# A decoder trunk on one NeuronCore: the roots of the head norms spread over the partitions by DMA instead of by matmul

## The reference, cut to what matters

```python
def _head_rmsnorm(y, g, n_heads):
    b, l, w = y.shape
    yh = y.reshape(b, l, n_heads, w // n_heads)
    yh = yh * lax.rsqrt(jnp.mean(yh * yh, axis=-1, keepdims=True) + NORM_EPS)
    return yh.reshape(b, l, w) * g.astype(F32)
...
    gates = jax.nn.sigmoid(merge_logits.reshape(b, l, N_BRANCH, D_MODEL) + b_merge.astype(F32))
    branches = (y_sb, y_gla, y_ml, y_ret)
    merged = gates[:, :, 0] * (branches[0] @ w_branch[0].astype(F32))
    for n in range(1, N_BRANCH):
        merged = merged + gates[:, :, n] * (branches[n] @ w_branch[n].astype(F32))
```

## Time and profile before

| | |
|---|---|
| Time, median of 3 runs | 978.7 us (978.58 to 979.68) |
| The profiled execution | 978.57 us |
| Its span in the trace | 976.4 us |
| Mean granted clock of TensorE | 0.998 |
| PE busy | 99% of the span |
| DVE busy | 60% |
| ACT busy | 52% |
| POOL busy | 8% |
| DMA queue of SP (q1) | 51% of 16 engines |

### The profile page before, as it was taken

One profiled execution on the slowest core, in us unless ns is written; L12 is line 12 of the kernel. 1 busy time (PEld: TensorE's weight loads), 2 busy tenths in 40 slices (PEclk: granted clock), 3 DMA queues, 4 the chain that ended last, 5 costly groups with the idle time before them and its releaser, 6 DMA issues.

```text
span 976.4 us, 19018 instructions
## 1 busy us (share of the span) xinstructions
PE 963.8 (99%) x7450; PEld 908.1 (93%) x7450; DVE 590.7 (60%) x894; ACT 512.5 (52%) x822; POOL 79.6 (8%) x72
## 2 busy tenths in 40 slices
PE   8999999999999999999999999999999999999998
PEld 6999888899999999999979999888999899999886
DVE  7566575367857655553456675654679566665543
ACT  6543744475466544444445546544754765544542
POOL 1000000000031222210100000000000312122000
PEclk9999999999999999999999999999999999999999
DMA  6875334346562655555544664433465635656652
GB/s 192 279 231 161 118 115 130 112 125 161 164 208 73 194 172 172 173 182 183 156 129 147 186 184 130 131 113 117 143 180 167 191 122 182 194 191 195 213 174 86
DMA packets 164299, 158.02 MB, mean 162 GB/s; under 512 B 9603, under 2 KB 157294, under 8 KB 163854
## 3 DMA queue, kind: packets, MB, share of 16 engines
q1 hardware_dynamic: 163118, 153.76, 51.0%
q10 hardware_dynamic: 928, 3.33, 1.0%
q0 software_dynamic: 192, 0.07, 0.0%
HBM read 154.98 MB, written 1.05 MB: 160 GB/s over the span
## 4 chain that ended last, share of the span: by engine, by line
PE 92%; DVE 4%; ACT 2%; DMA 1%; issue 1%; ACTq 0%; DVEq 0%; SPq 0%
PE banks L684 24%; PE banks L686 24%; PE banks L685 24%; PE banks L1059 2%; PE banks L1061 2%; PE banks L1060 2%; PE banks L734 2%; PE banks L719 1%; PE banks L715 1%; PE banks L716 1%; DVE lo L1521 1%; PE banks L926 1%; PE banks L924 1%; DVE term L1817 1%; PE banks L664 1%
## 5 line engine op out<-in xcount | busy, mean ns | idle before, releaser
L684 PE MATMUL banks<-xh,hi 128*128 128x272 f32 (+1 forms) x1584 | 457.2, 289 | 0.2
L1521 DVE TENSOR_TENSOR lo<-raw,hi 128x1024 fp32r<-128x1024 f32 (+1 forms) x288 | 349.0, 1215 | 174.1 <-ACT hi L1146 173.6
L686 PE MATMUL banks<-xh,lo 128*128 128x272 f32 (+1 forms) x1584 | 452.9, 286 | 0.0
L685 PE MATMUL banks<-xl,hi 128*128 128x272 f32 (+1 forms) x1584 | 451.9, 285 | 0.0
L1146 ACT ACTIVATE hi<-raw 128x1024 fp32r<-128x1024 f32 (+1 forms) x288 | 301.6, 1048 | 118.5 <-PE banks L686 43.2
L684 PEld LDWEIGHTS banks<-xh,hi 128*128 128x128 f32 x1584 | 298.5, 188 | 6.6 <-issue 4.7
L686 PEld LDWEIGHTS banks<-xh,lo 128*128 128x128 f32 x1584 | 298.6, 189 | 0.0
L685 PEld LDWEIGHTS banks<-xl,hi 128*128 128x128 f32 x1584 | 298.3, 188 | 0.0
L1236 ACT ACTIVATE gates<-banks,par 128x272 f32<-128x272 f32 (+1 forms) x64 | 30.7, 480 | 98.2 <-PE banks L686 91.1
L1967 POOL TENSOR_TENSOR silu_g<-silu_g,rstd 128x272 f32<-128x272 f32 (+1 forms) x44 | 54.6, 1240 | 216.7 <-ACT silu_g L1411 216.7
L1960 POOL TENSOR_TENSOR sq<-sq 128x272 f32<-128x272 f32 (+1 forms) x18 | 21.3, 1185 | 608.6 <-ACT sq L1396 608.0
(11 more groups left out here) (272 smaller groups left out, 1253.3 us busy)
## 6 DMA issues: line engine op xcount, KB each, us to landing
raw<-in_w_in SPq DMA_DIRECT2D x54, 1024.0 KB, 5.2
raw<-in_ffn_w_gate SPq DMA_DIRECT2D x22, 1024.0 KB, 5.3
raw<-in_ffn_w_up SPq DMA_DIRECT2D x22, 1024.0 KB, 5.3
raw<-in_ffn_w_down SPq DMA_DIRECT2D x19, 1024.0 KB, 5.1
raw<-in_w_out SPq DMA_DIRECT2D x8, 1024.0 KB, 5.1
raw<-in_w_in SPq DMA_DIRECT2D x12, 512.0 KB, 4.2
raw<-in_w_branch SPq DMA_DIRECT2D x12, 512.0 KB, 5.4
raw<-in_ffn_w_down SPq DMA_DIRECT2D x4, 768.0 KB, 4.4
```

Of the source, the lines that this page charges most:

```text
L684: mm(dst, wh, mh, start=start, stop=False)
L685: mm(dst, wh, ml, start=False, stop=False)
L686: return mm(dst, wl, mh, start=False, stop=stop)
L1521: tt(half_of(lo, g, c), half_of(raw, g, c), half_of(hi, g, c).bitcast(F32), ALU.subtract).then_inc(lo_ready, 2 if g in G_MIX else 1)
```

## The change

The selector matrix, its 768 columns of constants and the function `headbc` go away. In their place SP gets the function `spread_norms`. It waits for the roots, writes them by four DMAs (three rows of 272 numbers each) into a scratch `norm_rows` in device memory, waits until these have landed, and reads them back by four DMAs, each with a source that is repeated over 64 partitions, into a new SBUF tile `spread` of 128 x 6 x 272. `spread` lies where `pt` was, which is free once the last mixer's values are done (`o_ready`). `y_rest` waits for all four reads and takes `spread` from SBUF instead of a PSUM bank.

```diff
-          ("headsum", 3 * 32), ("headbc", 6 * P), ("denind", 32), ("negind", 4)]
+          ("headsum", 3 * 32), ("denind", 32), ("negind", 4)]
...
-    19: [("headbc",)],
...
+        (spread,), _ = tenants(merged_at, [("spread", [P, 6, T], F32)])
+        norm_rows = nc.dram_tensor("norm_rows", (DEPTH, HEADS, 3, T), F32, kind="Internal").ap()
...
+            def spread_norms(l):
+                sp.wait_ge(hrstd_ready, l + 1)
+                for g in range(HEADS):
+                    sp.dma_start(norm_rows[l, g], M["rows"][32 * g:32 * g + 3, 0, :]).then_inc(norm_moved, 16)
+                sp.wait_ge(norm_moved, 128 * l + 64)
+                sp.wait_ge(o_ready[l], 8)
+                for i in range(2):
+                    rows = slice(HD * i, HD * i + HD)
+                    sp.dma_start(spread[rows, 0:2, :], norm_rows[l:l + 1, i::2, 0, :].broadcast_to((HD, 2, T))).then_inc(norm_moved, 16)
+                    sp.dma_start(spread[rows, 2:6, :], norm_rows[l:l + 1, :, 1 + i, :].broadcast_to((HD, 4, T))).then_inc(norm_moved, 16)
...
                     load(G_LOGIT[l] + j // 2, wm[:, :, C_MERGE + n * D + m * P:C_MERGE + n * D + m * P + 256])
+                spread_norms(l)
                 for k in range(6):
...
-            def headbc(l):
-                pe.wait_ge(hrstd_ready, l + 1)
-                pe.wait_ge(sc_free[l], 4 * HEADS)
-                pe.wait_ge(ex_free[l], 2 * HEADS)
-                pe.wait_ge(k0_free[l], 4)
-                pe.wait_ge(den_abs, l + 1)
-                pe.wait_ge(o_free[l], 8)
-                for p in range(6):
-                    rows = slice(HD * p, HD * p + HD) if p < 2 else quad[p - 2]
-                    mm(spread_banks[p][:, 0:T], c3("headbc", 6)[rows, p, :], M["rows"][rows, 0, :], start=True, stop=True).then_inc(spread_ready[l], 1)
...
-                dve.wait_ge(spread_ready[l], p + 1)
-                stt(osb[:, n, q0:], osb[:, n, q0:], par[:, l, row + n % 2:row + n % 2 + 1], spread_banks[p][:, q0:T],
+                dve.wait_ge(norm_moved, 128 * l + 64 + 64)
+                stt(osb[:, n, q0:], osb[:, n, q0:], par[:, l, row + n % 2:row + n % 2 + 1], spread[:, p, q0:],
```

More of the change, by code:

```diff
@@ L89 @@
           ("decay", 4 * SCW), ("decay0", T), ("cos", T), ("sin", T),
-          ("headsum", 3 * 32), ("headbc", 6 * P), ("denind", 32), ("negind", 4)]
+          ("headsum", 3 * 32), ("denind", 32), ("negind", 4)]
 CONST_FIRST = 257
 CONST_W = sum(w for _, w in CONSTS)
-def head_row(pair, i):
-    return 32 * (2 * pair + i) if pair < 2 else 32 * (pair - 2) + 1 + i
 def constants():
@@ L131, in constants @@
     c["headsum"][:HD, 64 + 1] = c["headsum"][HD:, 64 + 2] = 1.0 / HD
-    for pair in range(6):
-        for i in range(P):
-            c["headbc"][head_row(pair, i // HD), pair * P + i] = 1
     c["denind"][:, 0] = 1
@@ L441, in turn_banks @@
             return (ops, k0) if name == "sbv" else (sc[0], sc[1])
-        spread_banks = [banks[:, 2 + p, :] for p in range(6)]
         branch_banks = [banks[:, 2 + 2 * i:4 + 2 * i, :] for i in range(3)]
@@ L459, in build @@
         row_summed = sq_ready[DEPTH - 1][3]
-        pair_done = sem("pair_done")
+        pair_done, norm_moved = sem("pair_done"), sem("norm_moved")
         ss_ready = sem("ss_ready")
@@ L465, in build @@
         names = """
-            rot_sin spread_ready spread_free sq_summed
+            rot_sin spread_free sq_summed
             silu_ready silu_scaled rstd_ready xn_ready xh_ready xl_ready post_scaled h_ready pad_set
@@ L472, in build @@
             ml_ready ah_ready al_ready turn_ready turn_free""".split()
-        (rot_sin, spread_ready, spread_free,
+        (rot_sin, spread_free,
          sq_summed, silu_ready, silu_scaled, rstd_ready, xn_ready, xh_ready, xl_ready, post_scaled, h_ready,
@@ L989, in _ @@
             parts = {
-                "first": first, "group": group, "turn": turn, "gate": gate, "logit": logit, "headsum": headsum, "headbc": headbc,
+                "first": first, "group": group, "turn": turn, "gate": gate, "logit": logit, "headsum": headsum,
                 "sb_scores0": sb_scores0, "sb_scores": sb_scores,
```

## The result

The changed kernel takes 994.21 us (median of 4 runs, 993.27 to 995.0), the kernel before 979.19 us beside it: a ratio of 1.0148, 95% interval 1.0136 to 1.0161. It is slower, as forecast, but by 15 us in place of 5.4. The profiled execution took 993.27 us; its span is 991.0 us, 14.6 more than before.

What follows compares the result with a forecast made beforehand. PE was taken as the bound, busy for 963.8 of 976.4 us. To 978.57 us the prediction added 1.5 and 2.3 for the longer layers, net of the gain, and 1.6 for the clock: 984.0 us, range 979.5 to 989.5.

Steps and rivals of the forecast that it cites:

- gain on PE: Logits 19 to 20, both layers: without the spread and its break PE gains 2 x 1.53 = 3.06 us.
- load issued to writes landed, layer 0: SP's queue: load issued at 200.96, the small writes behind it landed at 206.6, 0.5 us behind the load.
- reads: Four DMAs of together 836 KB into the spread tile: 4.8 us, bounds 4.2 and 6.5.
- tile to logit 20 taken: Layer 0, DVE and ACT: logit 20 is taken 2.94 us after the spread tile is there.
- standstills of PE: Ahead of logit 22: PE stands still 3.0 us in layer 0 and 3.9 us in layer 1.
- clock: Behind the standstills: one fall to the 1.2 GHz level for both layers, 1.6 us; bounds none and 3.2.
- the longer trip with two falls: Rival: writes at 207.4, reads of 6.5 us, tile at 213.9 and about 702.8, two falls; 990.6 us, chance 0.13.
- The hidden trip: Rival: tile there at 208.4 and 696.4, PE waits for nothing and the gain is whole; 975.5 us, chance 0.09.

Runs made afterwards that it cites:

- the kernel without a trip: Changed kernel without the eight DMAs, y_rest multiplying by a tile of ones once the roots are ready; 977.51 us, 0.9982 of the kernel before.
- the unused trip: Kernel before, selector matmuls kept, with the same eight DMAs added at the same place and only the much later merge waiting for them; 979.7 us, 0.9999.
- all ahead: Changed kernel with all eight DMAs issued ahead of the weight load of logits 24 and 25 in place of behind it; 983.41 us, 1.0045.
- plain source: Changed kernel with reads of the same shapes from 64 different rows of a weight matrix in place of the repeated scratch row; 992.35 us, 1.0125.
- two reads: Changed kernel with two reads in contiguous pieces of 6528 bytes in place of four, and eight small writes in place of four; 993.23 us, 1.0147.
- on POOL's queue: Changed kernel with all eight DMAs of the trip issued by POOL in place of SP, shapes and order unchanged; 990.07 us, 1.0112.
- half of the bytes: Changed kernel with its four reads cut to half their size, pairs of heads sharing rows; 987.9 us, 1.0094.
- first pairs first: Changed kernel with the reads for pairs 0 and 1 issued first, on their own semaphore, for which y_rest 0 and 1 wait; 984.91 us, 1.0053.
- POOL, first pairs first: Changed kernel with the trip on POOL's queue and the first two pairs' reads first, on their own semaphore; 983.6 us, 1.0039.
- all ahead, first pairs first: Changed kernel with all eight DMAs ahead of the load of logits 24 and 25 and the first two pairs read first, with their own wait; 982.8 us, 1.0027.
- writes ahead: Changed kernel with the four writes ahead of the load of logits 24 and 25 and the reads behind it, first pairs first; 979.96 us, 1.0003.
- writes and first pairs ahead: Changed kernel with writes, their wait and reads of pairs 0 and 1 ahead of the load of logits 24 and 25, other reads behind; 979.24 us, 0.9997.
- the run with matmuls of ones: Changed kernel with nine calls of the function that issues matmuls of ones on PE ahead of logit 22; 987.53 us, 1.0078.

## Why the prediction was wrong

The sign and the mechanism were right, a wait of PE at logit 22 in each layer and a slow clock behind it, and the sizes were not: 993.27 us for the profiled execution against 984.0, above the range. By its own terms:

| term | forecast | measured in the profile |
|---|---|---|
| gain on PE | 3.06 | 2.1 (976.4 - 974.3, the kernel without a trip) |
| load issued to writes landed, layer 0 | 5.6 | 5.9 |
| reads | 4.8 | 6.6 and 6.85 |
| tile to logit 20 taken | 2.94 | 2.81 |
| standstills of PE | 3.0 and 3.9 | 5.0 and 5.6 |
| clock | 1.6 | 6.0 |

**What the prediction saw.** PE followed from logit 22 on without standing still again. The loads weren't hurt, which the unused trip shows best. The writes landed 0.7 behind the load (forecast 0.5), and the packets show the reason that the text had, the place behind the load in SP's queue. The chain from the tile to the bank was right to 0.13 us.

**The reads: the first step that failed.** They were sized at 4.8 us, with 6.5 as the upper bound, and took more than that bound. The value was read off between the rows for 512 KB (4.2) and 1024 KB (5.1), which differ by 0.9 us for half a megabyte. The four issues were then counted only in the upper bound. Half the bytes show that these reads have a steeper slope, 1.7 and 1.3 us for 418 KB, and the rate row shows them at 184 to 264 GB/s where the weight load reaches 400, with the DMA engines as busy. The upper bound was itself built on the 512 KB row; the 6.2 us of the gain vector (a row of the view of all DMAs, not of the page) were at hand, for fewer bytes than the tile has, and were read only as the absence of a slow repetition. The runs exclude the repeated source, and larger pieces in fewer reads account for 0.7 to 0.9 us. What else nearly halves the rate stays open. With the writes, 0.3 us later against the load than forecast, the standstills become 3.7 us longer than forecast.

**The clock: the second step, and the larger.** The size of one fall was right: four stretches at the half level cost 6.0 us of busy time, 1.5 each, where 1.6 stood in the forecast. The number of falls was wrong. The text took one for both layers, with two as the upper bound, because the only row at hand showed a single stretch of 3.4 us; behind standstills of 5.0 and 5.6 us there were two stretches each. Either step alone would have stayed inside the range, 984.0 + 3.7 = 987.7 and 984.0 + 4.4 = 988.4; together they leave it. And they hang together: over the runs, the longer waits have the more stretches, though not one by one, for 3.2 us in one layer brought none and 2.2 us in another brought one. (All columns are in us; in the two rows "all ahead" the waits are those of all logit tiles of the layer.)

| kernel | waits at logit 22, layers 0 and 1 | at half clock | PE busy above 961.1 |
|---|---|---|---|
| changed | 5.0, 5.6 | 6.8, 6.8 | 6.0 |
| plain source | 5.3, 5.6 | 6.8, 6.8 | 5.5 |
| two reads | 5.1, 5.6 | 6.8, 6.8 | 5.0 |
| on POOL's queue | 5.1, 5.6 | 3.4, 6.8 | 3.4 |
| half of the bytes | 3.4, 4.4 | 3.4, 3.4 | 3.5 |
| first pairs first | 3.2, 3.2 | 0, 3.4 | 2.4 |
| POOL, first pairs first | 2.6, 3.0 | 0, 3.4 | 1.5 |
| all ahead | 2.5, 2.5 | 3.4, 0 | 2.3 |
| all ahead, first pairs first | 1.3, 2.2 | 0, 3.4 | 3.1 |
| writes ahead | 2.1, 1.1 | 0, 0 | 0.5 |
| writes and first pairs ahead | 0.7, 0.4 | 0, 0 | 1.2 |

The last column holds more than the clock, as the last two rows show (0.5 and 1.2 us without any fall), so the 1.5 per stretch is good to some tenths only; the run with matmuls of ones gives 6.7 / 4 = 1.7 by the medians and 5.4 / 4 = 1.4 by the profiled executions.

The Trainium skill, TensorE: Matmul & The Clock Gate, section "What's actually happening", has the half rate as the default that activity releases. The run with matmuls of ones agrees: the same 10.9 us of delay, no fall, 6.7 us less. The prediction quoted it and priced it at one fall more, so two in all, where four came.

**The gain.** The break between logits 19 and 20 was 1.53 us in each layer, and its removal brought 2.1 us of span and 2.0 of time. The term itself was sized right, since the logit tiles are 1.5 us shorter in each layer. The 1.0 us by which the span falls short lies elsewhere, 0.35 of it ahead of logit 18 of layer 0, 0.2 between the layers and 0.4 behind logit 26 of layer 1. The medians fall short by as much, so it isn't an accident of one profile; no run shows where it comes from.

**The rivals.** The nearest was the longer trip with two falls, 990.6, at a chance of 0.13: its tile at 213.9 for 214.44. Its clock term, too, was half of what came. The hidden trip had the estimate from the Trainium skill, DMA: Bandwidth & Descriptors, section "Anatomy of one DMA", of 5.9 us for writes and reads together. The section fits its 2.0 us and 436 GB/s to DMAs issued by GpSimd, which the prediction didn't say, and the trip here is issued by SP. Measured were 5.9 us from the load's issue to the landing of the writes alone, and 6.6 for the reads. Where nothing else was in flight, the four writes took 2.2 us from the first issue, and the last of them, issued at 202.60, had landed at most 1.2 us later, sooner than the page's 2.0 us; on POOL's queue beside a load they took 3.3 to 4.7 us each, more than it.

With the terms as measured the sum is 978.57 - 2.1 + 10.6 + 6.0 = 993.1 us, against 993.27. That is bookkeeping of the same profiles; what tests it are the run in which nobody waits and the one with matmuls of ones.

## What to carry to other kernels

Before a round trip through device memory takes the place of a broadcast on an engine, write down when its first and its last byte are needed: here the same eight DMAs cost 15 us against the kernel before where one wait was set for all of them behind a 1 MB load, and nothing where the writes and the first consumer's part stood ahead of that load and the rest behind it. Price a wait of PE together with the slow stretch behind it, since 10.6 us of waiting cost 16.6 here. And measure first what there is to gain: the kernel without any trip was only 2.0 us faster, so that even a well placed trip ended level.

## What the runs showed of the hardware

- Four DMAs of 3 KB issued on SP's queue right behind a 1 MB load moved as the load's last packets ran, and had landed 5.9 us after the load's issue; with no load in flight they took 2.2 us from the first issue. From POOL's queue, beside the load, the first landed after 3.3 us, ahead of the load, and the others after 4.4 to 4.7 us each.
- Four reads of together 836 KB, each over 64 partitions in pieces of 1088 bytes, ran at 184 to 264 GB/s where a load of 1 MB over 128 partitions reached 400 GB/s, with the DMA engines as busy (share 1.02 and 1.06). From issue to first use they took 6.6 and 6.85 us from a repeated source, 6.9 and 6.5 from a plain one.
- The half clock came in stretches of 3.4 us, none, one or two behind a standstill. Waits of nearly the same length gave one stretch or two (5.1 and 5.0 us, layer 0), and none or one (3.2 us in either layer of one run), so their number can't be foretold from the wait alone. The shortest wait with a fall behind it was 2.2 us.
